# Neighbourhood attention: four low weight parts on GpSimd, and an addition ahead of a scaling

## The reference, cut to what matters

```python
def second_block(x, p, g_mix, w_in, ...):
    h = x
    a = rms_norm_2(h, g_mix[i])
    qa, ka, va, qb, kb, vb = split(a @ w_in[i])
    oa = diff_attention(qa, ka, va, ...)              # 512 columns
    ob = neighbourhood_attention(qb, kb, vb, ...)     # 16 heads of 32, 512 columns
    h = h + jnp.concatenate([oa, ob], axis=-1) @ w_out[i]
    h = h + hier_moe(rms_norm_2(h, g_ffn[i]), ...)
    ...

def neighbourhood_attention(q, k, v, g_q, g_k, rpb):
    # 8 rows of 64 tokens; a block of 16 columns attends to 8 rows x 32 columns of keys
    def row_step(args):
        sc = jnp.einsum('bjqhd,bjkhd->bhjqk', qb, kg).astype(jnp.float32) * scale + bias
        pr = jax.nn.softmax(sc, axis=-1).astype(vg.dtype)
        o = jnp.einsum('bhjqk,bjkhd->bjqhd', pr, vg)
        ...
```

## Time and profile before

| what | value |
|---|---|
| median of 3 runs | 1568.12 us (1565.55 to 1568.25) |
| the profiled execution | 1564.59 us |
| its span, first to last instruction | 1562.9 us |
| mean granted TensorE clock | 0.999 |
| busy share of the span: PE, DVE, ACT, POOL | 97%, 46%, 34%, 11% |
| the attention steps in question | about 905 to 977 us of the span |

### The profile page before, as it was taken

How to read it: one execution, slowest core, us unless ns; L and a number is a source line. 1 busy time by engine, 2 the same in 40 slices (tenths; PEclk the granted TensorE clock), 3 DMA queues, 4 the chain that set the end, 5 groups by cost and what they waited for, 6 DMA issues and landing times.

```text
span 1562.9 us, 19660 instructions
## 1 busy us (share of the span) xinstructions
PE 1519.1 (97%) x7812; PEld 1062.7 (68%) x7812; DVE 717.7 (46%) x1210; ACT 528.6 (34%) x907; POOL 167.0 (11%) x174
## 2 busy tenths in 40 slices
PE   6999999999999999999999989999999999999998
PEld 6776788888888888888777766755444444444367
DVE  5346332465444444468665788541122132132174
ACT  5334422354232423345455587421100011010042
POOL 1024100002111111110300210020000000000000
PEclk9999999999999999999999999999999999999999
DMA  8111422312222222222110131889999999999951
GB/s 331 48 68 62 189 97 92 121 68 94 96 108 102 91 84 102 108 95 82 55 53 29 68 149 56 318 348 380 420 420 422 421 420 421 421 422 420 421 226 55
DMA packets 45613, 311.74 MB, mean 199 GB/s; under 512 B 5184, under 2 KB 5696, under 8 KB 10192
## 3 DMA queue, kind: packets, MB, share of 16 engines
q1 hardware_dynamic: 42480, 296.74, 47.4%
q0 software_dynamic: 3040, 13.72, 2.4%
HBM read 302.05 MB, written 8.39 MB: 199 GB/s over the span
## 4 chain that ended last, share of the span: by engine, by line
PE 87%; DVE 5%; ACT 4%; issue 2%; DMA 1%; SPq 0%; DVEq 0%; ACTq 0%
PE bank L803 21%; PE bank L2537 14%; PE bank L2553 7%; PE bank L1467 7%; PE bank L838 6%; PE bank L2520 4%; PE bank L855 4%; PE bank L2570 4%; PE bank L2729 3%; PE bank L1324 3%; PE bank L816 2%; PE bank L826 2%; PE bank L873 1%; PE bank L847 1%; DVE M L2174 1%
## 5 line engine op out<-in xcount | busy, mean ns | idle before, releaser
L627 DVE TENSOR_TENSOR w_lo<-M,w_hi 128x2048 fp32r<-128x2048 f32 x73 | 169.0, 2321 | 180.0 <-ACT w_hi L622 180.0
L2537 PE MATMUL bank<-M 128*64 128x512 f32 x1024 | 226.8, 595 | 1.7 <-ACT M L2625 1.0
L622 ACT ACTIVATE w_hi<-M 128x2048 fp32r<-128x2048 f32 x73 | 139.0, 1911 | 144.5 <-PE bank L803 56.9
L803 PE MATMUL bank<-HTH,w_hi 128*128 128x512 f32 x432 | 168.1, 389 | 0.0
L803 PE MATMUL bank<-HTL,w_hi 128*128 128x512 f32 x432 | 168.1, 389 | 0.0
L803 PE MATMUL bank<-HTH,w_lo 128*128 128x512 f32 x432 | 168.0, 389 | 0.0
L2537 PEld LDWEIGHTS bank<-M 128*64 128x64 f32 x1024 | 71.7, 137 | 135.7 <-issue 134.7
L2553 PE MATMUL bank<-M 128*64 128x512 f32 x512 | 113.6, 595 | 1.5 <-DMA M<-in_w 1.5
L2691 DVE TENSOR_TENSOR X<-bank,X 128x512 f32<-128x512 f32 x69 | 46.5, 688 | 109.7 <-PE bank L2570 109.6
L803 PEld LDWEIGHTS bank<-HTH,w_lo 128*128 128x128 f32 x432 | 81.1, 188 | 16.9
L803 PEld LDWEIGHTS bank<-HTH,w_hi 128*128 128x128 f32 x432 | 81.1, 188 | 16.8
(11 more groups left out here) (378 smaller groups left out, 2830.9 us busy)
## 6 DMA issues: line engine op xcount, KB each, us to landing
M<-in_w SPq DMA_DIRECT2D x192, 1024.0 KB, 10.9
M<-in_wd SPq DMA_DIRECT2D x78, 1024.0 KB, 4.8
M<-in_nb SPq DMA_DIRECT2D x4, 1536.0 KB, 6.7
X<-in_x SPq DMA_DIRECT2D x4, 512.0 KB, 7.4
M<-in_tb POOLq DMA_DIRECT2D x8, 256.0 KB, 4.4
M<-in_rows POOLq DMA_DIRECT2D x4, 512.0 KB, 6.7
rowb<-in_rows POOLq DMA_DIRECT2D x4, 512.0 KB, 5.8
xs_parts<-XSH POOLq DMA_DIRECT2D x1, 2048.0 KB, 9.8
```

The lines of the kernel that those rows point to most:

```text
L622: e.activation(hi[:, :], slots[slot_of[n]], ACT.Copy).then_inc(split_hi_done, 1)
L627: e.tensor_tensor(lo[:, :], slots[slot_of[n]], hi[:, :], ALU.subtract).then_inc(split_lo_done, 1)
L803: m = e.matmul(out[:, :], w[:, k0 + k, n0:n0 + 128], v[k], start=(k == 0 and i == 0), stop=(k == len(hi) - 1 and i == 2))
L2537: m = e.matmul(b[64 * s:64 * s + 64, :], Xe[:, 4 * kh + k, o + C * s:o + C * s + C], unit_w(key, 4)[:, k, :], start=(kh == 0 and k == 0), ...
```

## The change

It makes two edits, and renames `split_dve` to `split_low`. The low parts of the four `w_out` units move from VectorE's queue to GpSimd's: unit 0 behind the spread for group 2, units 2, 1 and 3 behind the spread for group 3. In VectorE's step the addition of a finished `o2a` tile moves from behind the scaling to ahead of it. Nothing else is added or taken away; what is computed stays the same.

```diff
@@ nbr_pool
                 spread(e, hg)
+                if hg == 2:
+                    split_low(e, unit["out2", 0])
+            for n in (2, 1, 3):
+                split_low(e, unit["out2", n])
@@ nbr_dve
                 for v in VJ_DVE.get(i, ()):
                     evac_dve(e, Vj[:, v, :], ("vj", v))
+                if i in O2A_SUM:
+                    out2_add(e, "o2a", *O2A_SUM[i])
                 if i == 2:
                     oa_lo_dve(e, OA_AT[0])
@@ nbr_dve
                 if i == 2:
                     oa_lo_dve(e, OA_AT[2])
-                if i - 1 in O2_SPLIT:
-                    split_dve(e, unit["out2", O2_SPLIT[i - 1]])
-                if i in O2A_SUM:
-                    out2_add(e, "o2a", *O2A_SUM[i])
                 if i >= 3 and NBR[i - 3][1] == 3:
```

More of the change, by code:

```diff
@@ L622, in split_act, with split_low @@
             e.activation(hi[:, :], slots[slot_of[n]], ACT.Copy).then_inc(split_hi_done, 1)
-        def split_dve(e, n):
+        def split_low(e, n):
             hi, lo = split_bufs(n)
@@ L632, in next_split_act, with next_split_low @@
             split_act(e, unit[key] + NSPLIT)
-        def next_split_dve(e, key):
-            split_dve(e, unit[key] + NSPLIT)
+        def next_split_low(e, key):
+            split_low(e, unit[key] + NSPLIT)
         def split_ready(e, key):
@@ L979, in pre_dve @@
                 if step == "split":
-                    split_dve(e, 0)
+                    split_low(e, 0)
                 else:
                     norm_dve(e, 0, *step)
-            split_dve(e, 1)
-            split_dve(e, 2)
+            split_low(e, 1)
+            split_low(e, 2)
         def pre_pe(e):
@@ L1025, in proj_dve @@
             evac_dve(e, kT[:, 0, :], ("k", 0))
-            next_split_dve(e, ("in", 0))
+            next_split_low(e, ("in", 0))
         def proj_pool(e):
@@ L1212, in att_dve @@
                 if i in A_SPLIT:
-                    next_split_dve(e, A_SPLIT[i])
+                    next_split_low(e, A_SPLIT[i])
                 if i in PL_AT:
@@ L1335, in gate_dve @@
         def gate_dve(e):
-            next_split_dve(e, ("ga", 0))
+            next_split_low(e, ("ga", 0))
             e.wait_ge(a_pv, len(ATT))
@@ L1339, in gate_dve @@
                 if i:
-                    next_split_dve(e, ("ap", i))
+                    next_split_low(e, ("ap", i))
                 for q, name in enumerate(("ga", "gb")):
@@ L1347, in gate_dve @@
                     if i == q == 0:
-                        next_split_dve(e, ("ap", 0))
+                        next_split_low(e, ("ap", 0))
                     elif q == 0 or i < 3:
-                        next_split_dve(e, (name, i))
+                        next_split_low(e, (name, i))
                     if i == 3 and q == 0:
@@ L1357, in gate_dve @@
                 e.tensor_tensor(HTL[:, n, :], MT[:, n, :], HTH[:, n, :], ALU.subtract).then_inc(mt_lo, 1)
-            next_split_dve(e, ("gb", 3))
+            next_split_low(e, ("gb", 3))
         def gate_pool(e):
@@ L1405, in wo_dve @@
         def wo_dve(e):
-            next_split_dve(e, ("wo", 0))
-            next_split_dve(e, ("wo", 1))
+            next_split_low(e, ("wo", 0))
+            next_split_low(e, ("wo", 1))
             e.wait_ge(mt_lo, 8)
@@ L1412, in wo_dve @@
                 if t == 3 and s == 0:
-                    next_split_dve(e, ("wo", 2))
-            next_split_dve(e, ("wo", 3))
+                    next_split_low(e, ("wo", 2))
+            next_split_low(e, ("wo", 3))
         def wo_pool(e):
@@ L1524, in ffn_dve @@
                     if u == 0:
-                        next_split_dve(e, ("uv", 0))
+                        next_split_low(e, ("uv", 0))
                     for n in (2 * u, 2 * u + 1):
                         if u and n % 2:
-                            next_split_dve(e, ("uv", u))
-                            next_split_dve(e, ("ug", u))
+                            next_split_low(e, ("uv", u))
+                            next_split_low(e, ("ug", u))
                         conv_dve(e, ("ug", n), ZG[n % 4], 22 + n, 2 * n + 1)
@@ L1532, in ffn_dve @@
                     if u == 0:
-                        next_split_dve(e, ("ug", 0))
+                        next_split_low(e, ("ug", 0))
                 if s < LAST:
@@ L1544, in ffn_dve @@
                     for d in ds:
-                        next_split_dve(e, ("dn", d))
+                        next_split_low(e, ("dn", d))
         def ffn_pool(e):
@@ L1568, in ffn_end_dve @@
                 if t == 3 and s == 0:
-                    next_split_dve(e, ("dn", 9))
-            next_split_dve(e, ("dn", 10))
+                    next_split_low(e, ("dn", 9))
+            next_split_low(e, ("dn", 10))
         def ffn_end_pool(e):
@@ L1688, in qk_dve @@
                 u = 4 if G is None else 2 * G
-                next_split_dve(e, ("in2", u))
+                next_split_low(e, ("in2", u))
                 for n in range(TT + 2):
@@ L1698, in qk_dve @@
                         if n == TT:
-                            next_split_dve(e, ("in2", u + 1))
+                            next_split_low(e, ("in2", u + 1))
                         if n >= 2:
                             rope_dve(e, 4 * G + n - 2)
-            next_split_dve(e, ("in2", 5))
+            next_split_low(e, ("in2", 5))
         def qk_sum_dve(e, x):
@@ L2008, in dif_dve @@
                 if i in SPLIT_AT:
-                    next_split_dve(e, ("in2", SPLIT_AT[i]))
+                    next_split_low(e, ("in2", SPLIT_AT[i]))
                 if i - 1 in ROOT_AT:
@@ L2816, in end_dve @@
             norm_dve(e, 4, 1, 4)
-            split_dve(e, unit["plg", 0])
+            split_low(e, unit["plg", 0])
             sums(3)
             gains(3)
-            split_dve(e, unit["plg", 1])
+            split_low(e, unit["plg", 1])
             norm_dve(e, 4, 2, 4)
             norm_dve(e, 4, 3, 4)
-            split_dve(e, unit["plg", 2])
+            split_low(e, unit["plg", 2])
             for t in range(TT):
@@ L2829, in end_dve @@
             dve_own.mark(e.reciprocal(r, sq))
-            split_dve(e, unit["plg", 3])
+            split_low(e, unit["plg", 3])
             e.wait_ge(dve_own.sem, dve_own.n)
```

## The result

The changed kernel takes 1568.14 us, median of 12 runs (1565.52 to 1570.48); the kernel before takes 1565.91 us, median of 12 runs on the same chip (1563.64 to 1568.25). The ratio is 1.0016, 95% interval [1.0009, 1.0024], which is +2.5 us on 1566. The kernel after is slower by a little that the interval tells from nothing (+1.4 to +3.8 us), and by less than the 0.2% that the prediction took as no change. The forecast of +2.9 us lies inside the interval. The profiled execution took 1567.35 us against 1564.59, with a span of 1565.5 against 1562.9.

What follows compares the result with a forecast made beforehand. TensorE, busy 97% of the span, was taken as the bound, with VectorE nearly as tight in the attention steps. The terms 2.9 - 1.2 + 0.9 + 0.3 = +2.9 us on 1568.12 gave 1571.0 us, range 1565.0 to 1574.5.

Steps and rivals of the forecast that it cites:

- The price of a low part on GpSimd: One 128x2048 subtraction on GpSimd: 4.60 us, scaled from a quarter-size row, with bounds of 3.56 and 5.17 us.
- the second rival: GpSimd's queue: from about 4.65 us a part, unit 3 and the gain load wait; +5.2 us, 1573.3 us; chance 0.40.
- The hold for the whole instruction: VectorE operations reading two SBUF tensors, and the small negation, stand until GpSimd's instruction of about 4.6 us is over.
- The first rival: GpSimd's hold on VectorE is short or absent for so long an instruction: -3.3 us at best, 1564.8 us; chance 0.20.
- Unit 0, +2.9 at step 8: Steps 3 to 8: GpSimd's low part holds VectorE's negation 4.5 us, delaying the scores by 2.9 us at step 8.
- One sign: If the forecast was right, TensorE would be idle some 3 us ahead of the transposes of item 2.
- The addition, -1.2: Step 8: the addition of tile (1, 0), ahead of the scaling, starts 1.14 us earlier, ending TensorE's 1.27 us wait: -1.2.
- The rival that it gives nothing: TensorE reaches the bank late after the first hold, so -1.2 is missing: +4.1, 1572.2 us; counted within the second rival.
- Unit 2, +0.9: Steps 13 to 15: the negation stands until 962.45, delaying exponentials, copies and TensorE's second half of the transposes by 0.9 us.
- Units 1 and 3, +0.3: Two low parts in a row on GpSimd end at 982.1; TensorE needs the second at 981.85: +0.3 us.
- The sum: The terms of unit 0, the addition, unit 2 and units 1 and 3 together: +2.9 us, reaching the end in full.
- the forecast case alone: Whole hold at 3.6 to 4.65 us a part: +0.5 to +3.1 us, 1568.6 to 1571.2 us; chance 0.40.

Runs made afterwards that it cites:

- four pieces: The changed kernel with each low part made by four GpSimd instructions of 512 columns in place of one of 2048; 1564.82 us, ratio 0.9993.
- addition alone: The kernel before with only the addition moved ahead of the scaling, all four low parts staying on VectorE; 1564.82 us, ratio 0.9997.
- the last two: The kernel before with the addition ahead and unit 2's low part one step later, without and with unit 0's in pieces on GpSimd; ratios 0.9992 and 0.9988.
- units 1 and 3: The kernel before with the addition ahead and only the low parts of those two units on GpSimd; 1564.76 us, ratio 0.9999.
- unit 2 alone: The kernel before with the addition ahead and only that unit's low part on GpSimd; 1565.2 us, ratio 0.9995.
- unit 0 alone: The kernel before with the addition ahead and only that unit's low part on GpSimd; 1566.87 us, ratio 1.0007.

## Why the prediction was right, point by point

- **The price of a low part on GpSimd** was taken as 4.60 us, from 3.56 to 5.17. Measured, from the instructions by line (count, busy us, mean ns):

```profile
L627 POOL TENSOR_TENSOR w_lo<-M,w_hi 128x2048 fp32r<-128x2048 f32 x4 | 18.4, 4598 | 35.6 <-ACT w_hi L622 35.6
```

  The value from the quarter-size row and the fixed part was right to 2 ns; the line to the second rival, 4.65 us, was only 0.05 us away. The GPSIMD Engine Reference of the Trainium skill, section 3.1, gave 4497 ns for an addition; this subtraction took 0.10 us more, so the measurement decides for the row. By the prediction's own rule that 0.10 us counts four times, its estimate of the sum at that price is +2.5, not +2.4.

- **The hold for the whole instruction.** The prediction had rows for 1.07 us at most and chose the whole length. It stood 4.52 us, and with pieces 1.22: right, and shown by the kernel with four pieces. The section "SBUF: two separate sides" of SBUF — State Buffer in the Trainium skill gives the shared ports to whichever starts first, a GpSimd operation or a VectorE operation of the kinds that it names, for the whole instruction. The trace agrees, at 4.52 us. The first rival (short or absent hold, 1564.8 us) is out. That the operations which read PSUM go free was assumed; they took 0.42 us beside GpSimd.

- **Unit 0, +2.9 at step 8.** Measured +2.64 from item 3 to item 8. The walk gave 920.9 for the scores of item 5, the trace 920.69; between there and step 8 TensorE gained back 0.4 (2.91 late at item 5, 2.49 at item 8), and the estimate between VectorE's +2.3 and TensorE's +3.1 should have lain a quarter of a us lower. One sign did not come as written: TensorE was to be idle some 3 us ahead of the transposes of item 2. It waited 1.69 us there and 0.73 ahead of the product with the values, 2.4 in all; TensorE's work ahead of that wait had been stretched into it by the lower clock from 911 on: from the scores of item 4 to the end of the pieces it took 4.16 us (912.45 to 918.30 - 1.69), before 3.02 (912.59 to 915.61).

- **The addition, -1.2.** Measured -1.29 in after, -1.30 alone. The rival that it gives nothing is out.

- **Unit 2, +0.9.** The chain of waits was right (the negation until 961.78, forecast 962.45, then the copies, then the second half of the transposes), the term was mis-sized: +0.59. Two small slips make that up. The prediction compared the end of the stand (962.45) with the start of the undisturbed negation (961.53), so its own 0.17 us was counted as delay. And against the scaling ahead of it, which came 1.18 us later than before (956.10 against 954.92), GpSimd's part began at 957.14 - 1.18 = 955.96, where the forecast, with its shift of 1.7, had 957.85 - 1.7 = 956.15: 0.19 sooner. The forecast let GpSimd wait for the end of VectorE's scaling; but it began 0.15 us behind the high part (956.99), as at unit 0 (912.33 behind 912.18), while the record of the scaling runs to 957.32. That the scaling holds GpSimd there is not shown.

- **Units 1 and 3, +0.3.** TensorE reached the first product with unit 3 0.26 us later than its earlier delay explains, and the last product of the four units 0.40 us later (23.01 against 22.61 in the last column). The gain row's load was issued at 981.18, forecast 982.14, and VectorE waited 0.93 us for it where before it waited 2.40; nothing came of it. A row of after on VectorE:

```profile
989.74 1.28 DVE L700 SCALAR_TENSOR_TENSOR M<-X,st,M 128x1024 f32<-128x1024 f32 x1 [0.93 <-DMA M<-in_rows]
```

  So the second rival, slower by a dearer queue, is out: its price did not come.

- **The sum.** Forecast 2.9 - 1.2 + 0.9 + 0.3 = +2.9; the same terms measured in the trace: 2.64 - 1.29 + 0.59 + 0.40 = +2.34, less 0.15 by which the stage began earlier: +2.19 at the last product of the four units. The end of the span is +2.6. The last +0.4 needs no cause: from that product to the end, where the code is the same in all, before takes 563.2 us and after 563.7, and the profiles of the other eight kernels take from 561.9 to 564.8. So the terms of the holds were too high by some 0.6 us, and that the total came within 0.4 us is in part luck.

- **The absolute time** was 1571.0, measured 1568.14. The difference between the kernels was right to 0.4 us; what was off is the base. The prediction added the sum to 1568.12, the median of three runs, and noted that the profiled execution was 3.5 us below it. The 12 runs of before have a median of 1565.91: the three lay high, and the profiled one was the more typical. So 1568.14 lies below the range of the forecast case alone (1568.6 to 1571.2); it lies inside the stated range (1565.0 to 1574.5) because that range also covers the rivals, and it would have covered no change as well.

## What to carry to other kernels

A large elementwise instruction moved from VectorE to GpSimd does not only cost its own 4.6 us; here it held a VectorE instruction of 128x4 elements until its end. So the price is what waits for the first held instruction behind its start, here that negation with the exponentials behind it: 2.6 us for unit 0, where that came at once, and 0.6 us for unit 2, where VectorE's scores, which read PSUM, ran meanwhile. Cutting the instruction into pieces shortens the stand to one piece: with the addition ahead in both, the four low parts made the kernel 2.5 us slower whole and 1.1 us faster in pieces (the second interval reaches to +0.3). The pieces take away the loss and no more: no run here shows that a low part on GpSimd gains anything over the addition alone (0.9993 against 0.9997 with all four in pieces). Moving such work to a later place in the queue of its own engine (0.6 us in the ledger here, too little for the times) is to be tried before moving it to another engine.

## What the runs showed of the hardware that was not expected

**The clock after a short wait.** At about 907.8 TensorE waits 2.5 us for a scaling in the kernel before, in the kernel after, and in the addition alone. What follows differs from one profiled execution to another. Windows of 1 us (length, PE, PEld, DVE, ACT, POOL, then the granted clock, DMA share, GB/s), after and then the addition alone:

```profile
910.00:911.00 1.00, 0.69 (x6) 0.70 (x7) 1.00 (x3) 1.00 (x2) 0.94 (x2) 1.00 0.00 0
911.00:912.00 1.00, 1.00 (x16) 0.69 (x18) 1.00 (x7) 1.00 (x1) 0.39 (x1) 0.58 0.00 0
912.00:913.00 1.00, 1.00 (x14) 0.57 (x8) 0.89 (x3) 0.18 (x1) 0.67 (x1) 0.50 0.00 0
...
915.00:916.00 1.00, 1.00 (x6) 0.78 (x6) 1.00 (x1) 0.00 (x0) 1.00 (x1) 1.00 0.00 0
```

```profile
909.00:910.00 1.00, 0.00 (x0) 0.00 (x0) 1.00 (x1) 1.00 (x3) 0.94 (x2) 0.57 0.00 0
910.00:911.00 1.00, 0.69 (x3) 0.69 (x4) 1.00 (x3) 1.00 (x2) 0.94 (x2) 0.50 0.00 0
...
915.00:916.00 1.00, 1.00 (x4) 0.67 (x3) 1.00 (x1) 0.64 (x2) 0.00 (x0) 0.52 0.00 0
916.00:917.00 1.00, 1.00 (x6) 0.82 (x5) 1.00 (x6) 0.00 (x0) 0.00 (x0) 1.00 0.00 0
```

The granted clock falls to 0.50, which is 1.2 of 2.4 GHz, for some 3 us in the one and nearly 7 us in the other, where it falls while TensorE still waits; in the profiled executions of before and of the four pieces it stays at 1.00 there, with the same wait. In the other eight of the ten profiled kernels it falls, in the last two already at about 907.0 and 905.7, where TensorE's longest wait in the 5 us before was 0.8 us. Rows of TensorE behind that wait, the addition alone and then four pieces:

```profile
910.31 1.97 PE L2100 MATMUL bank<-cst,M 128*128 128x128 f32 x8 [2.56 <-DVE M L2198]
```

```profile
910.24 1.09 PE L2113 MATMUL bank<-cst,M 128*128 128x128 f32 x8 [2.57 <-DVE M L2211]
```

The same eight transposes take 1.97 us instead of 1.09. What a fall costs shows in three kernels that have the same queues up to step 12: from item 3 to 8, units 1 and 3 takes 23.21 us with some 3 us of lower clock, addition alone 24.33 and unit 2 alone 24.53 with nearly 7 us each. So the longer fall costs at least 1.1 us more than the shorter one, most of what the addition gives. After and unit 0 alone have the addition ahead and the shorter fall as units 1 and 3 has; their 25.96 is 2.75 us above its 23.21, so unit 0's +2.64 is not the clock's. Whether an edit changes how often the clock falls there, or the executions simply differ, is open: each kernel has one profile. A difference of 1 us in a single profile of this kernel can be the clock alone.
